# A full-precision decoder layer on one core: the eleventh gate-and-up chunk, and a sixth k-pair of the second down pass, by seven block products

## The chip, the cores and the metric

The kernel runs on one core of a Trainium2 chip. The metric is the device time of one execution in microseconds (us): median, lowest and highest of three runs. TensorE is called PE here, VectorE DVE, ScalarE ACT, GpSimd POOL and SyncE SP, as in the profile.

## The reference, cut to what matters

A sequence of 256 tokens with 2048 channels goes through a SwiGLU network, a token mixer and a second SwiGLU network, each followed by a layer norm. Only the two SwiGLU networks are touched here:

```
def swiglu(x, w_gate, w_up, w_down):
    return (jax.nn.silu(x @ w_gate) * (x @ w_up)) @ w_down

h = layer_norm(DEEPNORM_ALPHA * h + 0.5 * swiglu(h, w_gate, w_up, w_down), g, b)
```

`w_gate` and `w_up` are 2048 by 5632, `w_down` is 5632 by 2048, everything in float32.

## The kernel before, in words

**Products.** Each float32 operand is split into a high part and a rest, and a product of two tiles is three matmuls (high by high, high by rest, rest by high; the function `three`, and the three calls in `up_slab`, L882 to L884), each with 128 rows of tokens and 512 columns of weights. A *slab* is a piece of a weight matrix of two k-tiles (256 rows) by 512 columns, 512 KB. Used plainly it takes 2 k-tiles x 2 token tiles x 3 = 12 matmuls.

**Seven products.** Two slabs with the same rows (gate and up, or two neighbouring column blocks of the down matrix) make, with the two k-tiles and the two token tiles, a 2 by 2 block product. It can be had with seven products instead of eight: 21 matmuls for a pair of slabs where the plain way has 24 (`seven_products`). For that DVE forms three sums of weight tiles (`block_sums`, L2020 to L2025), which ACT and DVE split in high and rest (`t_high_part` L1486, `t_low_part` L2031), and four mixes of token tiles, once for a k-pair (`mixed_of` L1979 to L1985, `mixed_high` L1453, `mixed_low` L2011). The seven results go to eight PSUM banks: `own` holds results by column and token tile, `aux` four partial results, which DVE adds in when the last block is done: `copy_one` and `collect` (L2037 to L2039), `sum_chunk` (L1955, L1957), `product_summed` (L1962) for a chunk, `copy_one_down` and `collect_down` (L2106 to L2114) for a down pass.

**The stages.** Gate and up go over 11 chunks of 512 hidden columns, 16 slabs each. `acc` and `spare`, four banks each, take turns as a chunk's `own`. Chunk 0 is plain, chunks 1 to 9 (`NC_S` = 9) have k-pairs 2, 4 and 6 by seven products (`up_seven`), and chunk 10 is plain (`up_plain`). After a chunk DVE multiplies silu(gate) by up, PE transposes the product (`turn_hidden`, eight small matmuls at L895) and ACT and DVE split it into `g_hi` and `g_lo` (L1432, L1970). The down projection then goes over the 22 k-pairs of the hidden columns in two passes (j = 0 and 1), each for two blocks of 512 output columns, so 44 slabs; `DOWN_ORDER` gives the order of the k-pairs and `DOWN_SEVEN` = 11, 13, 15, 17, 19 those by seven products in both passes. In pass 0 these stand in the last half, slabs 22 to 41; in pass 1 they alternate with plain pairs from slab 8 on. Both networks run the same code (f = 1 and 2).

**What sets the order.** The program of each engine is written out by slab number l. SP loads slab l into one of four landing places as soon as DVE is done with slab l - 4 (L507). ACT copies it to `w_hi` (L1343) when it has landed and PE is done with slab l - 4. DVE forms `w_lo` (L1787), and PE waits for that. All other work of ACT and DVE stands in front of the split of some slab. In down pass 0 DVE has, in front of the split of the slab named:

- slab 3: the product of chunk 10 (`product_plain`, L1949); slab 7: `hidden_low`
- slabs 10, 12, 14, 16: one quarter of the residual. In the first network it is one multiplication (L2142), in the second `prepare_rows` (L1871, L1873), which waits for quarters and for `rows`, the gain and bias of a layer norm, both loaded by POOL
- slabs 11, 13, 15, 17, 19: `mixed_down`, the mix of one of the five k-pairs, behind the `mixed_low` of the one before; slab 21: the last `mixed_low`

POOL loads the residual again once its space, which holds the chunks' partial sums, is free: the upper half when the last seven-product chunk is summed (`refill_late`, L655), the lower half when the last chunk is transposed (L659, L739). In the second network it loads `rows` between the two (L627, L628), at the end of chunk 10.

Of the kernel before, what the change touches and what calls it, by code (L numbers as in the profile page):

```python
# [90 lines left out]
DOWN_SLABS = [[(p, 1 - c if DOWN_ORDER[j][p] in DOWN_SEVEN else c) for p, c in DOWN_SLABS[j]] for j in range(2)]  # L91
UP_BLOCKS = NC_S * len(SEVEN)
ALL_BLOCKS = UP_BLOCKS + 2 * len(DOWN_SEVEN)
# [110 lines left out]
def down_block(f, j, q):  # L204
    return (f - 1) * ALL_BLOCKS + UP_BLOCKS + j * len(DOWN_SEVEN) + q

# [67 lines left out]
def build_decoder_layer(nc, x, positions, ffn1_w_gate, ffn1_w_up, ffn1_w_down, ln1_g, ln1_b, w_in, conv_w, conv_b,  # L274
# [20 lines left out]
    with ctx:  # L295

        land_all = sb("land", [P, 3 + LAND * 2, W])
        t_sums = land_all[:, 0:3, :]
        land = land_all[:, 3:3 + LAND * 2, :].rearrange("p (r k) n -> p r k n", r=LAND)
# [13 lines left out]
        def placed(name, shape, dt, at):  # L313
# [40 lines left out]
        sz = sb("sz", [P, TOK, W])  # L354
        bcT = sb("bcT", [P, 2, SEQ])
# [32 lines left out]
        t_of = {"up": (t_hi, t_lo), "down": (d_t_hi, d_t_lo)}  # L388
# [104 lines left out]
        def _(sp):  # L493
# [28 lines left out]
            def up_rest(f, phase):  # L522
                with sp.Fori(1, NC_S + 1) as i:
                    up_seven(f, phase, i)
                for i in range(NC_S + 1, NC_F):
                    up(f, phase, i)
# [219 lines left out]
        def _(pe):  # L746
# [157 lines left out]
            def seven_products(n, slab_at, l, rows_of, mixed, t_set, own, aux, first, last, turned=None):  # L904
# [7 lines left out]
                def t_block(m):  # L912
                    hi, lo = t_of[t_set]
                    return hi[:, m, :], lo[:, m, :]
# [14 lines left out]
            def up_seven_block(f, i, b, own, aux):  # L929
# [3 lines left out]
                def rows_of(k, t):  # L933
# [3 lines left out]
                               (s_hi[s], s_lo[s]), "up", own, aux, s == 0, s == len(SEVEN) - 1,  # L937
# [17 lines left out]
            def down_seven_block(f, j, l, own, aux):  # L955

                s = DOWN_ORDER[j][DOWN_SLABS[j][l][0]]
                q = DOWN_SEVEN.index(s)

                def rows_of(k, t):  # L960
                    return tuple(m[:, 2 * s + k, t * P:(t + 1) * P] for m in (g_hi, g_lo))

                if j == 0:
                    pe.wait_ge(mix_out, (f - 1) * MIXED + len(SEVEN) + q + 1)
                seven_products(down_block(f, j, q), slab_no(f"down{f}", j, l), l, rows_of, d_s[q], "down",
                               own, aux, q == 0, q == len(DOWN_SEVEN) - 1)

            def down(f):

                for j in range(2):  # L970
                    own, aux = chunk_banks(1 - j), chunk_banks(j)
                    if j == 0:
                        pe.wait_ge(gt_out, 2 * chunk_no(f, NC_F - 1))
                    else:
                        pe.wait_ge(aux_out, shared_down(f, 0) + 1)
                    for l, (p, c) in enumerate(DOWN_SLABS[j]):
# [5 lines left out]
                        if s in DOWN_SEVEN:  # L982
# [19 lines left out]
            def banks_drained(f, i):  # L1002
# [4 lines left out]
                n = shared_no(f, NC_S) + 1 if isinstance(i, int) and i > NC_S else shared_no(f, i)  # L1007
# [25 lines left out]

            def up_plain(f, i):

                for l in range(16):
                    if l == 0:
                        banks_drained(f, i)
                    if l == 4:
                        turn_hidden(f, i - 1, (i - 1) % 2)  # L1040
                    up_slab(f"up{f}", i, l, l % 8, l // 8, chunk_banks(i % 2), l % 8 == 0, l % 8 == 7)
# [16 lines left out]
            def ffn(f, ln, x_no):  # L1058
# [10 lines left out]
                for i in range(NC_S + 1, NC_F):  # L1069
                    up_plain(f, i)  # L1070
# [263 lines left out]
        def _(act):  # L1334
# [134 lines left out]
            def up_plain(f, i):  # L1469
                for l in range(16):  # L1470
                    if i == NC_S + 1 and l == 1:
                        copy_one(f, i - 1, (i - 1) % 2)
                    if i == NC_S + 1 and l == 4:
                        silu_summed(f, i - 1)
                    if l == 6:
                        hidden_high(f, i - 1, (i - 1) % 2)
                    if l == 10:
                        silu_plain(f, i)
                    split(f"up{f}", i, l)

            def t_high_part(n, t_set):
# [4 lines left out]
                act.activation(t_of[t_set][0][:, :, :], t_sums, ACT.Copy).then_inc(t_high, 1)  # L1486
# [6 lines left out]
            def up_seven(f, i, odd):  # L1493

                for l in range(16):
# [10 lines left out]
                    if n is not None and l % 2 == 1:  # L1506
                        t_high_part(n, "up")

            def ffn(f, ln, cols):
# [6 lines left out]
                for i in range(NC_S + 1, NC_F):  # L1516
                    up_plain(f, i)
                down(f)

            def copy_one_down(f, j):  # L1520

                act.wait_ge(t_used, down_block(f, j, len(DOWN_SEVEN) - 1) + 1)
# [4 lines left out]
            def down(f):  # L1527
                for j in range(2):
                    for l, (p, c) in enumerate(DOWN_SLABS[j]):
                        s = DOWN_ORDER[j][p]  # L1530
                        if j == 0 and l == 6:
                            hidden_high(f, NC_F - 1, (NC_F - 1) % 2)
                        if j == 0 and l in (13, 15, 17, 19, 21):
                            mixed_high(f, len(SEVEN) + (l - 13) // 2)
                        if (j, l) == (1, 0):
                            copy_one_down(f, 0)
                        if (j, l) == (1, 30):
                            copy_one_down(f, 1)
                        n = down_block(f, j, DOWN_SEVEN.index(s)) if s in DOWN_SEVEN else None
# [3 lines left out]
                        if n is not None and l % 2 == 1:  # L1543
                            t_high_part(n, "down")
# [236 lines left out]
        def _(dve):  # L1781
# [216 lines left out]
            def mixed_down(f, q):  # L1998

                s = DOWN_SEVEN[q]  # L2000
                if q == 0:
                    dve.wait_ge(gt_out, 2 * chunk_no(f, NC_F - 1))
                    dve.wait_ge(t_rest, (f - 1) * ALL_BLOCKS + UP_BLOCKS)
                at = slice(2 * s, 2 * s + 2)
# [22 lines left out]
            def t_low_part(n, t_set):  # L2027

                hi, lo = t_of[t_set]
                dve.wait_ge(t_high, n + 1)  # L2030
                dve.tensor_tensor(lo[:, :, :], t_sums, hi[:, :, :].bitcast(F32), ALU.subtract).then_inc(t_rest, 1)  # L2031
# [27 lines left out]
            def up_plain(f, i):  # L2059
                for l in range(16):  # L2060
                    if i == NC_S + 1:
                        if l == 1:
                            collect(f, i - 1, (i - 1) % 2)
                        if l == 3:
                            sum_chunk(f, i - 1, (i - 1) % 2)
                        if l == 4:
                            product_summed(f, i - 1)
                    elif l == 2:
                        product_plain(f, i - 1)
                    if l == 7:  # L2070
                        hidden_low(f, i - 1, (i - 1) % 2)
                    split(f"up{f}", i, l)

            def up_seven(f, i, odd):
                for l in range(16):
# [21 lines left out]
                    if l // 2 in SEVEN and l % 2 == 1:  # L2097
                        t_low_part(seven_block(f, i, l // 2), "up")
# [29 lines left out]
            def down(f):  # L2128
                phase = f"down{f}"
                for j in range(2):  # L2130
                    for l, (p, c) in enumerate(DOWN_SLABS[j]):
                        s = DOWN_ORDER[j][p]
                        if j == 0 and l == 3:
                            product_plain(f, NC_F - 1)
                        if j == 0 and l == 7:
                            hidden_low(f, NC_F - 1, (NC_F - 1) % 2)
                        if j == 0 and l in (10, 12, 14, 16):
                            at = (2, 3, 0, 1)[(l - 10) // 2]
# [6 lines left out]
                        if j == 0 and l in (11, 13, 15, 17, 19, 21):  # L2145
# [476 lines left out]
```

## Time and profile before

| | |
|---|---|
| median of 3 runs | 2660.63 us (2659.67 to 2660.86) |
| the profiled execution | 2659.08 us, of which the span is 2657.5 us |
| mean granted TensorE clock | 0.998 |
| PE, DVE, ACT busy | 99%, 75%, 51% of the span |
| gate and up, then down, first network | from the start to about 718 us |
| gate and up, then down, second network | about 1938 us to the end |

PE is busy nearly all the time and the others are not. "Busy" counts a matmul from its issue to its modelled end, 0.39 us, while the next starts after 0.227 us; so a pause of PE of under 0.16 us does not show as idle time, and of a longer one 0.16 us are missing. The median of the runs is 1.55 us above the profiled execution.

### The profile page before, as it was taken

What the parts mean: (1) busy time and instruction counts of PE and PEld (TensorE: products, weight loads), DVE (VectorE), ACT (ScalarE), POOL (GpSimd) and SP (SyncE); (2) the same over time, 40 slices, a digit from 0 to 9 for tenths busy, and PEclk for the clock granted to TensorE, in tenths of its full rate; (3) what the DMA queues carried; (4) which work ended last, traced back from release to release, by engine and by line L of the source; (5) the groups of instructions that cost most, each with busy time, mean ns of one, the idle gap of its engine ahead of it and who ended that gap; (6) DMA issues with size and microseconds to landing.
All of it is one profiled execution on the core that took longest, in us unless ns stands there. A gap on an engine that the chain in (4) does not pass through costs nothing.

```text
span 2657.5 us, 36251 instructions
## 1 busy us (share of the span) xinstructions
PE 2634.0 (99%) x12570; PEld 2187.5 (82%) x12570; DVE 1982.3 (75%) x2254; ACT 1352.8 (51%) x1636; POOL 129.5 (5%) x170
## 2 busy tenths in 40 slices
PE   9999999999999999999999999999999999999997
PEld 7888888888887788888888888888888888888886
DVE  6988987688666665677777765444788989877886
ACT  4555555454444554566555554444365555554553
POOL 1000000000000000211111100000000000000000
PEclk9999999999999999999999999999999999999999
DMA  7666566666655546665555555667666666666664
GB/s 225 202 193 205 190 199 212 212 200 198 204 171 150 152 149 198 206 182 179 178 178 174 181 180 165 191 191 247 202 211 200 191 204 195 200 203 230 212 205 171
DMA packets 286466, 513.95 MB, mean 193 GB/s; under 512 B 19664, under 2 KB 53120, under 8 KB 284320
## 3 DMA queue, kind: packets, MB, share of 16 engines
q1 hardware_dynamic: 279824, 485.03, 58.5%
q0 software_dynamic: 4880, 25.36, 2.6%
q10 hardware_dynamic: 1664, 2.26, 0.2%
q8 instruction: 61, 1.00, 0.1%
q14 instruction: 37, 0.30, 0.0%
HBM read 506.23 MB, written 6.36 MB: 193 GB/s over the span
## 4 chain that ended last, share of the span: by engine, by line
PE 96%; DVE 3%; ACT 1%; issue 0%; DMA 0%; POOLq 0%; ACTq 0%; POOL 0%; SPq 0%; DVEq 0%
PE acc L796 13%; PE acc L798 13%; PE acc L797 13%; PE acc L900 5%; PE acc L901 5%; PE acc L902 5%; PE acc L882 5%; PE acc L884 5%; PE acc L883 5%; PE spare L900 4%; PE spare L902 4%; PE spare L901 4%; PE spare L882 3%; PE spare L884 3%; PE spare L883 3%; PE spare L765 2%
## 5 line engine op out<-in xcount | busy, mean ns | idle before, releaser
L1787 DVE TENSOR_TENSOR w_lo<-land,w_hi 128x1024 fp32r<-128x1024 f32 (+1 forms) x956 | 1152.3, 1222 | 517.7 <-ACT w_hi L1343 509.2
L1343 ACT ACTIVATE w_hi<-land 128x1024 fp32r<-128x1024 f32 (+1 forms) x956 | 967.4, 1026 | 927.9 <-PE acc L798 320.4
L796 PE MATMUL acc<-w_hi,a_hi 128*128 128x512 f32 (+1 forms) x1168 | 443.9, 380 | 1.0 <-DVE w_lo L1787 0.8
L798 PE MATMUL acc<-w_hi,a_lo 128*128 128x512 f32 (+1 forms) x1168 | 428.9, 367 | 0.0
L797 PE MATMUL acc<-w_lo,a_hi 128*128 128x512 f32 (+1 forms) x1168 | 427.5, 366 | 0.0
L796 PEld LDWEIGHTS acc<-w_hi,a_hi 128*128 128x128 f32 x1168 | 220.4, 189 | 44.7 <-issue 10.0
L798 PEld LDWEIGHTS acc<-w_hi,a_lo 128*128 128x128 f32 x1168 | 220.2, 189 | 37.5
L797 PEld LDWEIGHTS acc<-w_lo,a_hi 128*128 128x128 f32 x1168 | 220.7, 189 | 36.5 <-issue 3.6
L882 PE MATMUL acc<-w_hi,a_hi 128*128 128x512 f32 x560 | 220.0, 393 | 0.8 <-DVE w_lo L1787 0.7
L884 PE MATMUL acc<-w_hi,a_lo 128*128 128x512 f32 x560 | 218.2, 390 | 0.0
L883 PE MATMUL acc<-w_lo,a_hi 128*128 128x512 f32 x560 | 217.9, 389 | 0.0
L882 PE MATMUL spare<-w_hi,a_hi 128*128 128x512 f32 x400 | 156.5, 391 | 0.0
L884 PE MATMUL spare<-w_hi,a_lo 128*128 128x512 f32 x400 | 155.7, 389 | 0.0
L883 PE MATMUL spare<-w_lo,a_hi 128*128 128x512 f32 x400 | 155.7, 389 | 0.0
L882 PEld LDWEIGHTS acc<-w_hi,a_hi 128*128 128x128 f32 x560 | 105.1, 188 | 23.4 <-DVE w_lo L1787 1.1
L884 PEld LDWEIGHTS acc<-w_hi,a_lo 128*128 128x128 f32 x560 | 105.1, 188 | 22.2
L883 PEld LDWEIGHTS acc<-w_lo,a_hi 128*128 128x128 f32 x560 | 105.2, 188 | 21.2
L900 PE MATMUL spare<-w_hi,g_hi 128*128 128x512 f32 x292 | 114.0, 390 | 0.6 <-DVE w_lo L1787 0.6
L900 PE MATMUL acc<-w_hi,g_hi 128*128 128x512 f32 x292 | 113.7, 389 | 0.0
L901 PE MATMUL spare<-w_lo,g_hi 128*128 128x512 f32 x292 | 113.6, 389 | 0.0
L902 PE MATMUL spare<-w_hi,g_lo 128*128 128x512 f32 x292 | 113.6, 389 | 0.0
L902 PE MATMUL acc<-w_hi,g_lo 128*128 128x512 f32 x292 | 113.6, 389 | 0.0
(388 smaller groups left out, 4264.7 us busy)
## 6 DMA issues: line engine op xcount, KB each, us to landing
land<-w_in SPq DMA_DIRECT2D x232, 512.0 KB, 3.8
land<-ffn_w_gate SPq DMA_DIRECT2D x176, 512.0 KB, 4.0
land<-ffn_w_up SPq DMA_DIRECT2D x176, 512.0 KB, 4.1
land<-ffn_w_down SPq DMA_DIRECT2D x176, 512.0 KB, 4.5
land<-w_ssd_o SPq DMA_DIRECT2D x64, 512.0 KB, 4.0
land<-w_in SPq DMA_DIRECT2D x132, 128.0 KB, 2.3
land<-w_attn_o SPq DMA_DIRECT2D x32, 512.0 KB, 4.2
land<-w_out SPq DMA_DIRECT2D x32, 512.0 KB, 4.6
```

Of the source, the lines that this page charges most:

```text
L765: return pe.transpose(spare[0:src.shape[-1], bank, at:at + rows], src, ident[0:rows, 0:rows])
L796: pe.matmul(to, rows_hi, hi, start=first, stop=False)
L797: pe.matmul(to, rows_hi, lo, start=False, stop=False)
L798: mm = pe.matmul(to, rows_lo, hi, start=False, stop=last)
L882: pe.matmul(to, rows_hi, hi, start=first and k == 0, stop=False)
L883: pe.matmul(to, rows_hi, lo, start=False, stop=False)
L884: mm = pe.matmul(to, rows_lo, hi, start=False, stop=last and k == 1)
L900: pe.matmul(to, rows[0], block[0], start=first, stop=False)
L901: pe.matmul(to, rows[0], block[1], start=False, stop=False)
L902: return pe.matmul(to, rows[1], block[0], start=False, stop=last)
L1343: act.activation(w_hi[:, l % SPLIT, 0:deep, 0:width], land[:, l % LAND, 0:deep, 0:width], ACT.Copy).then_inc(high, 1)
L1787: dve.tensor_tensor(w_lo[:, l % SPLIT, 0:deep, 0:width], land[:, l % LAND, 0:deep, 0:width], w_hi[:, l % SPLIT, 0:deep, 0:width].bitcast(F ...
```

## The change

Chunk 10 also takes k-pairs 2, 4 and 6 by seven products (`NC_S` = 10), so no plain chunk is left behind the loop. Its partial results are collected, summed and multiplied in down pass 0, in front of the splits of slabs 1, 3 and 4, and PE waits for the collection before slab 0 of the pass, whose banks it fills. The down projection gets a sixth k-pair by seven products, k-pair 10, in pass 1 alone; it takes place 14 in the order, slabs 28 and 29, and its mix is formed in front of slab 5 of pass 1, with the `mixed_low` in front of slab 7. Pass 1's partial results are collected in front of slab 34 instead of 30. In pass 0 the four quarters of the residual move from slabs 10, 12, 14, 16 to 12, 14, 16, 18. The upper half of the residual is loaded again after the sum of chunk 10 and no longer in chunk 10. The split weight sums have one pair of buffers, `t_hi` and `t_lo`, for both stages, outside the shared region; in return `sz` and `bcT` lie on the sums' own space. The six mixes of the down projection lie at 88 to 112 K. Constants and places:

```diff
-NC_S = 9
-DOWN_SEVEN = (11, 13, 15, 17, 19)
-DOWN_ORDER = (tuple(range(22)), (0, 1, 2, 3, 11, 4, 13, 5, 15, 6, 17, 7, 19, 8, 9, 10, 12, 14, 16, 18, 20, 21))
+NC_S = 10
+DOWN_SEVEN = (11, 13, 15, 17, 19, 10)
+DOWN_BLOCKS = (5, 6)
+DOWN_ORDER = (tuple(range(22)), (0, 1, 2, 3, 11, 4, 13, 5, 15, 6, 17, 7, 19, 8, 10, 9, 12, 14, 16, 18, 20, 21))
+DOWN_COLLECT = 34
+MIX_FIRST, MIX_LATE = 11, 5
...
-ALL_BLOCKS = UP_BLOCKS + 2 * len(DOWN_SEVEN)
+ALL_BLOCKS = UP_BLOCKS + sum(DOWN_BLOCKS)
...
+        sz = land_all[:, 0:2, :]
+        bcT = land_all[:, 2, :].rearrange("p (k n) -> p k n", k=2)
...
-        sz = sb("sz", [P, TOK, W])
-        bcT = sb("bcT", [P, 2, SEQ])
...
-        t_hi = placed("t_hi", [P, 3, W], F32R, 36 * K)
-        t_lo = placed("t_lo", [P, 3, W], F32R, 80 * K)
+        t_hi = sb("t_hi", [P, 3, W], F32R)
+        t_lo = sb("t_lo", [P, 3, W], F32R)
...
-               for k, at in enumerate((88, 92, 108, 112, 116))]
-        d_t_hi = placed("d_t_hi", [P, 3, W], F32R, 96 * K)
-        d_t_lo = placed("d_t_lo", [P, 3, W], F32R, 102 * K)
+               for k, at in enumerate((88, 92, 96, 100, 104, 108))]
```

On PE, in `down` and `down_seven_block` (`up_plain` goes):

```diff
                     if j == 0:
                         pe.wait_ge(gt_out, 2 * chunk_no(f, NC_F - 1))
+                        pe.wait_ge(aux_out, shared_no(f, NC_S) + 1)
...
-                if j == 0:
-                    pe.wait_ge(mix_out, (f - 1) * MIXED + len(SEVEN) + q + 1)
+                pe.wait_ge(mix_out, (f - 1) * MIXED + len(SEVEN) + q + 1)
```

On ACT, in `down`:

```diff
-                        if j == 0 and l == 6:
-                            hidden_high(f, NC_F - 1, (NC_F - 1) % 2)
-                        if j == 0 and l in (13, 15, 17, 19, 21):
-                            mixed_high(f, len(SEVEN) + (l - 13) // 2)
+                        if j == 0 and l == 1:
+                            copy_one(f, NC_S, NC_S % 2)
+                        if j == 0 and l == 4:
+                            silu_summed(f, NC_S)
+                        if j == 0 and l == HIDDEN_AT:
+                            hidden_high(f, NC_S, NC_S % 2)
+                        if j == 0 and l in range(MIX_FIRST + 2, MIX_FIRST + 2 * DOWN_BLOCKS[0] + 2, 2):
+                            mixed_high(f, len(SEVEN) + (l - MIX_FIRST - 2) // 2)
+                        if j == 1 and l == MIX_LATE + 2:
+                            mixed_high(f, len(SEVEN) + DOWN_BLOCKS[0])
...
-                        if (j, l) == (1, 30):
+                        if (j, l) == (1, DOWN_COLLECT):
                             copy_one_down(f, 1)
```

On DVE, in `down`:

```diff
+                        if j == 0 and l == 1:
+                            collect(f, NC_S, NC_S % 2)
                         if j == 0 and l == 3:
-                            product_plain(f, NC_F - 1)
-                        if j == 0 and l == 7:
-                            hidden_low(f, NC_F - 1, (NC_F - 1) % 2)
-                        if j == 0 and l in (10, 12, 14, 16):
-                            at = (2, 3, 0, 1)[(l - 10) // 2]
+                            sum_chunk(f, NC_S, NC_S % 2)
+                        if j == 0 and l == 4:
+                            product_summed(f, NC_S)
+                        if j == 0 and l == HIDDEN_AT:
+                            hidden_low(f, NC_S, NC_S % 2)
+                        if j == 0 and l in (12, 14, 16, 18):
+                            at = (2, 3, 0, 1)[(l - 12) // 2]
...
+                        if (j, l) == (1, MIX_LATE):
+                            mixed_down(f, DOWN_BLOCKS[0])
+                        if (j, l) == (1, MIX_LATE + 2):
+                            mixed_low(f, len(SEVEN) + DOWN_BLOCKS[0])
...
-                        if (j, l) == (1, 30):
+                        if (j, l) == (1, DOWN_COLLECT):
                             collect_down(f, 1)
```

## Rows read from the trace of the kernel before

**Rows 1.** The page: busy time of each engine, share of the span, instructions.

```profile
PE 2634.0 (99%) x12570; PEld 2187.5 (82%) x12570; DVE 1982.3 (75%) x2254; ACT 1352.8 (51%) x1636; POOL 129.5 (5%) x170
```

**Rows 2.** Who PE waited for, 2400 us to the end: in total, times, longest (us).

```profile
PE spare L900 <- DVE w_lo L1787: 0.6, 1, 0.6
```

**Rows 3.** Timeline of PE: first matmuls of chunks 8, 10, down pass 0 (f = 1).

```profile
355.05 0.39 PE L882 MATMUL acc<-w_hi,a_hi 128*128 128x512 f32 x1
...
439.83 0.39 PE L882 MATMUL acc<-w_hi,a_hi 128*128 128x512 f32 x1
...
484.27 0.39 PE L900 MATMUL spare<-w_hi,g_hi 128*128 128x512 f32 x1
```

**Rows 4.** Busy time by stretch: us, then PE, PEld, DVE, ACT, POOL, PEclk, DMA share, GB/s.

```profile
2280.00:2320.00 40.00, 40.00 (x182) 33.17 (x181) 35.97 (x35) 21.74 (x22) 0.00 (x0) 1.00 0.64 201
2412.00:2416.00 4.00, 4.00 (x21) 3.32 (x20) 1.97 (x2) 1.06 (x1) 0.00 (x0) 1.00 0.99 412
```

**Rows 5.** Timeline of DVE at the start of chunk 10 (f = 1): start, us.

```profile
436.66 1.22 DVE L2039 TENSOR_TENSOR resid<-acc,resid 128x1024 f32<-128x1024 f32 x1
...
440.07 1.21 DVE L1955 TENSOR_TENSOR resid<-resid,spare 128x1024 f32<-128x1024 f32 x1
441.20 1.21 DVE L1957 TENSOR_TENSOR resid<-resid,spare 128x1024 f32<-128x1024 f32 x1
...
443.59 1.22 DVE L1962 TENSOR_TENSOR resid<-resid 128x1024 f32<-128x1024 f32 x1
```

**Rows 6.** Timeline of DVE in down pass 0 (f = 2), slabs 9 to 18.

```profile
2426.01 1.23 DVE L1787 TENSOR_TENSOR w_lo<-land,w_hi 128x1024 fp32r<-128x1024 f32 x1 [1.49 <-ACT w_hi L1343]
2427.16 1.22 DVE L1871 SCALAR_TENSOR_TENSOR resid<-resid,rows 128x1024 f32<-128x1024 f32 x1
...
2429.67 1.23 DVE L1787 TENSOR_TENSOR w_lo<-land,w_hi 128x1024 fp32r<-128x1024 f32 x1
2430.81 0.68 DVE L1979 TENSOR_TENSOR sz<-g_hi,g_lo 128x512 f32<-128x512 f32 x1
...
2432.53 1.22 DVE L1787 TENSOR_TENSOR w_lo<-land,w_hi 128x1024 fp32r<-128x1024 f32 x1
...
2437.31 0.68 DVE L2011 TENSOR_TENSOR d_lo<-sz,d_hi 128x512 fp32r<-128x512 f32 x1
...
2439.75 1.22 DVE L1787 TENSOR_TENSOR w_lo<-land,w_hi 128x1024 fp32r<-128x1024 f32 x1
...
2454.21 2.35 DVE L1787 TENSOR_TENSOR w_lo<-land,w_hi 128x1024 fp32r<-128x1024 f32 x2
```

**Rows 7.** Timeline of PE (f = 2): start of down pass 0, and around slab 17.

```profile
2407.45 0.39 PE L900 MATMUL spare<-w_hi,g_hi 128*128 128x512 f32 x1
...
2454.53 0.39 PE L902 MATMUL spare<-w_hi,g_lo 128*128 128x512 f32 x1
2455.48 0.50 PE L900 MATMUL spare<-w_hi,g_hi 128*128 128x512 f32 x1 [0.56 <-DVE w_lo L1787]
2455.82 0.40 PE L901 MATMUL spare<-w_lo,g_hi 128*128 128x512 f32 x1
```

**Rows 8.** Timeline at slab 22 (f = 2): DVE's sums and split, PE's first seven-product block.

```profile
2463.97 1.23 DVE L2020 TENSOR_TENSOR land<-land 128x1024 f32<-128x1024 f32 x1 [0.96 <-DMA land<-ffn_w_down]
2466.57 2.35 DVE L1787 TENSOR_TENSOR w_lo<-land,w_hi 128x1024 fp32r<-128x1024 f32 x2
...
2469.21 0.39 PE L900 MATMUL spare<-w_hi,d_hi 128*128 128x512 f32 x1
```

**Rows 9.** DMA issues, 2405 to 2430 us: count, KB each, median us to landing.

```profile
land<-ffn_w_down SPq DMA_DIRECT2D x8, 512.0 KB, 5.9
rows<-ln_g POOLq DMA_DIRECT2D x1, 1024.0 KB, 7.4
rows<-ln_b POOLq DMA_DIRECT2D x1, 1024.0 KB, 10.0
```

**Rows 10.** Timeline of DVE: residual in pass 0 (f = 1); slab 6 of pass 1 (f = 2).

```profile
503.98 0.68 DVE L2142 TENSOR_SCALAR resid<-resid 128x1024 f32<-128x1024 f32 x1
...
2535.16 1.23 DVE L1787 TENSOR_TENSOR w_lo<-land,w_hi 128x1024 fp32r<-128x1024 f32 x1 [1.08 <-ACT w_hi L1343]
```

More of the change, by code:

```diff
@@ L902, in three, with seven_products @@
                 return pe.matmul(to, rows[1], block[0], start=False, stop=last)
-            def seven_products(n, slab_at, l, rows_of, mixed, t_set, own, aux, first, last, turned=None):
+            def seven_products(n, slab_at, l, rows_of, mixed, own, aux, first, last, turned=None):
                 def block(l, k):
@@ L936, in up_seven_block @@
                 seven_products(seven_block(f, i, b), slab_no(f"up{f}", i, 2 * b), 2 * b, rows_of,
-                               (s_hi[s], s_lo[s]), "up", own, aux, s == 0, s == len(SEVEN) - 1,
+                               (s_hi[s], s_lo[s]), own, aux, s == 0, s == len(SEVEN) - 1,
                                chunk_no(f, i) * 2 if s == 0 else None)
@@ L961, in rows_of @@
                     return tuple(m[:, 2 * s + k, t * P:(t + 1) * P] for m in (g_hi, g_lo))
-                if j == 0:
-                    pe.wait_ge(mix_out, (f - 1) * MIXED + len(SEVEN) + q + 1)
-                seven_products(down_block(f, j, q), slab_no(f"down{f}", j, l), l, rows_of, d_s[q], "down",
-                               own, aux, q == 0, q == len(DOWN_SEVEN) - 1)
+                pe.wait_ge(mix_out, (f - 1) * MIXED + len(SEVEN) + q + 1)
+                seven_products(down_block(f, j, q), slab_no(f"down{f}", j, l), l, rows_of, d_s[q],
+                               own, aux, q == 0, q == DOWN_BLOCKS[j] - 1)
             def down(f):
@@ L1006, in banks_drained @@
                     pe.wait_ge(gt_out, n)
-                n = shared_no(f, NC_S) + 1 if isinstance(i, int) and i > NC_S else shared_no(f, i)
+                n = shared_no(f, i)
                 if not is_zero(n):
@@ L1467, in up_first, with t_high_part @@
                     split(phase, 0, l)
[L1469 to L1481, printed above, removed]
+            def t_high_part(n):
                 act.wait_ge(sums, n * 3 + 3)
@@ L1485, in t_high_part @@
                     act.wait_ge(t_used, n)
-                act.activation(t_of[t_set][0][:, :, :], t_sums, ACT.Copy).then_inc(t_high, 1)
+                act.activation(t_hi[:, :, :], t_sums, ACT.Copy).then_inc(t_high, 1)
             def copy_one(f, i, odd):
@@ L1515, in ffn @@
                         up_seven(f, m * 2 + (ALONE - 1 + k), (ALONE + 1 + k) % 2)
[L1516 to L1517 removed]
                 down(f)
             def copy_one_down(f, j):
[L1522 removed]
+                act.wait_ge(t_used, down_block(f, j, DOWN_BLOCKS[j] - 1) + 1)
                 if j == 1:
@@ L1543, in down @@
                         if n is not None and l % 2 == 1:
-                            t_high_part(n, "down")
+                            t_high_part(n)
             ffn(1, "xT", None)
@@ L2057, in up_first @@
                 mixed_low(f, len(SEVEN) - 1)
[L2059 to L2072, printed above, removed]
             def up_seven(f, i, odd):
@@ L2164, in down @@
                         if n is not None and l % 2 == 1:
-                            t_low_part(n, "down")
+                            t_low_part(n)
                 evacuate_down(f, 1, 0)
```

49 lines of the change are left out of this document (19 added, 30 removed).

## The prediction, made before the changed kernel ran

> **What bounds the kernel now.** I read the page first: PE is busy 99% of the span, DVE 75%, ACT 51% [rows 1]. Then the list of waits. In the second network's last chunk and both its down passes PE waited once, 0.6 us, for DVE's `w_lo` [rows 2]. Then the timeline of PE. Chunks 8 and 9, seven-product chunks, take 439.83 - 355.05 = 84.78 us, 42.39 each; plain chunk 10 takes 484.27 - 439.83 = 44.44 [rows 3]. A plain chunk has 16 x 12 = 192 large matmuls, a seven-product one 5 x 24 + 3 x 21 = 183, and both have eight transposes. So nine matmuls make 2.05 us, 0.228 each, and PE sets the time. DVE is close behind: in a stretch of seven-product chunks it is busy 35.97 of 40 us and PE all 40 [rows 4]. So the questions are how many matmuls go, and whether DVE stays ahead where work is put on it.
>
> **How far DVE is ahead.** DVE can be no more than four slabs ahead, since `w_hi` of slab l waits for PE to be done with slab l - 4. In down pass 0 of the second network it waits for ACT, and ACT for PE, up to slab 9 (split at 2426.01, 1.49 us idle before it), and is free at 2427.16 [rows 6]. PE starts slab 0 at 2407.45 and slab 17 would have started at 2454.53 + 0.23 = 2454.76 [rows 7], so it reaches slab 9 eight slabs of 2.72 us earlier, at 2433.0. DVE's lead is thus 5.8 us when full. From there it falls.
>
> **Removed.** Per network: three blocks in chunk 10 and one in pass 1, each three matmuls. That is 2 x (3 + 1) x 3 = 24 matmuls. Six blocks in chunk 10 are 2 x 2.05 = 4.10 us; six matmuls in pass 1 at 0.228 are 1.36. Sum 5.46 us. Bounds: 24 matmuls at 0.226 to 0.230 give 5.4 to 5.5.
>
> The rule that speaks against this size is in the Trainium skill, TensorE: Matmul & The Clock Gate, section Back-to-back issue gap. It gives 131 ns for a sustained matmul of 512 columns, about 216 ns for an isolated one; by these the 24 would be worth, as an estimate, 3.1 or 5.2 us. The trace disagrees with both.
>
> **Added in chunk 10 and at the head of pass 0.** DVE gets the block sums of chunk 10 (three times the pattern of rows 8: 2.60 us of sums and a split of the sums), then the collection, two sums and the product. All this is what it does in chunks 1 to 9, where PE loses nothing [rows 4]: the first sum starts 0.24 us after PE enters the next stage (440.07 against 439.83) and the product ends at 444.8 [rows 3, 5]. PE wants the product for the transposes in front of slab 3, 3 x 2.72 = 8.2 us after its entry, so 3.2 us are left. The new wait of PE in front of slab 0 is for the collection, whose last instruction ends at 437.88, 2.0 us before PE would stop [rows 3, 5]. Behind that wait stands all of PE's work, so late here is late one for one; but the last plain pair of chunk 10 (5.4 us) covers it as it covers chunks 1 to 9. Cost 0, bounds 0 and 0.3. By slab 9 the lead is full again, since plain slabs leave DVE 1.5 us each [rows 6].
>
> **The middle of pass 0, second network.** This is the term that costs. Steps, from rows 6: a split takes DVE 1.14 us (2429.67 to 2430.81). A quarter of the residual with its split takes 2429.67 - 2427.16 + 1.14 = 3.65. The first mix with its split takes 2432.53 - 2430.81 + 1.14 = 2.86. A later one, with the `mixed_low` before it, takes 2439.75 - 2437.31 + 1.14 = 3.58. PE takes 2.72 for each.
> Before, DVE has quarters at 10, 12, 14, 16 and mixes at 11, 13, 15, 17: 28.3 us from 2427.16, so the split of slab 17 ends at about 2455.43 where PE wanted it at 2454.76. PE starts at 2455.48 and its next matmul follows after 0.34 instead of 0.23 us [rows 7], 0.85 us lost. From 18 on there is no quarter and DVE recovers.
> After, the quarters are at 12, 14, 16, 18 and the mixes stay. Slab 10 is split on the beat and leaves DVE free at 2426.01 + 2.72 + 1.14 = 2429.87. To the end of slab 18 it has 2.86 + 4 x 3.65 + 3 x 3.58 = 28.2 us, hence 2458.1, and 0.1 for the split's own end; PE wants slab 18 at 2457.48 and loses 0.85. Then slab 19 has another mix: 3.58 against 2.72, 0.86 lost again. Sum 1.7, against 0.85 before: **0.87 us more.** In both networks the number of such instructions is the same; what is new is that the last mix follows the last quarter directly.
> At slab 22 the block sums wait for a landing [rows 8]. Slab 23 can be asked for only when slab 19 is split, so with DVE at its latest this chain moves too: split 22 ended at about 2467.8 for a PE start at 2469.21, 1.4 us to spare; sums move by 1.5 us, PE by 0.87, which leaves 0.8. Cost 0, bounds 0 and 0.8, if the landing takes as much longer as it did under load.
> Bounds of this whole term: 0 and 1.7. In the first network a quarter is one instruction of 0.68 us [rows 10], so a quarter and a mix take 0.72 + 1.14 + 3.58 = 5.44 us for two slabs, which is PE's time: 0.
>
> **Pass 1.** The mix of k-pair 10 adds 1.72 us in front of slab 5 and its `mixed_low` 0.7 in front of slab 7. At slab 6 DVE waits for ACT, that is for PE, 1.08 us, and at slab 7 again [rows 10]; the lead of some 5 us covers both. Cost 0, without that cover up to 2.4 a network. The collection at 34 stands four slabs behind its last block, as at 30 before. 0.
>
> **POOL's transfers.** The upper half of the residual (1 MB) is now asked for about 2 us into pass 0, in front of `rows` (2 MB); all wait for SP's stream too. In the second network they share 412 GB/s [rows 4], of which the slabs, 0.524 MB each 2.72 us, need 193. `rows` landed 7.4 and 10.0 us after their issue [rows 9]. One more MB at some 210 GB/s is 5 us: the last row would land at about 2426, before DVE wants it at slab 12, at 2432.7. Cost 0. SP's slabs took a median of 5.9 us to land there [rows 9] and made nobody wait. SP's and ACT's other steps only change place.
>
> **Sum.** -5.46 + 0.87 = -4.6 us. Profiled execution 2659.08 to about 2654.5 (span 2652.9); median of the runs 2660.63, 1.55 above it, to **2656.0**. That is 0.17% faster, inside the 0.2% (5.3 us) that a measurement of this kernel can tell from no change.
>
> **Rivals.**
> *The full saving.* DVE makes up the second late mix, or the landing of the quarters lets it start sooner. For it: only 0.87 us are at stake. Against it: the steps of rows 6 are the same every time. Time 2655.2, a bare 0.2% faster. Chance 0.14.
> *Pauses in the first blocks too.* The landing for slab 23 comes late, and DVE, busy at 90%, gains only some tenths of a microsecond a block, so that two or three pauses follow. Price 1 to 3 us over the forecast: 2657 to 2659. For it: 0.96 us idle for a landing already [rows 8]. Chance 0.14.
> *Slower.* The late quarters or `rows` aren't there at slab 12. From there DVE has no slack, so each us is lost by PE. To be slower by 5.3 us, `rows` must land at about 2432.7 + 9.9 = 2442.6, that is POOL's 3.1 MB must move at under 100 GB/s from 2411. At 90 GB/s they land at 2446: -5.46 + 0.87 + 13.8 = +9.2, 2669.8. Against it: 412 - 193 = 219 GB/s went to POOL's transfers [rows 4]. Chance 0.02. The Trainium skill, DMA: Bandwidth & Descriptors, section Queues, rings and completion order, says that an engine takes its queues in turn, a packet from each; by that POOL's queue can't be starved.
> *It doesn't do what it says.* Then no block is gained and the time stays; the diff leaves no room for it. Chance 0.01.
>
> **How the numbers follow.** Forecast 0.69. Range 2654.7 to 2658.3: below, the full saving and the runs' own spread of 0.6; above, 1.7 us for the middle of pass 0 and a pause at slab 22. Faster by over 0.2% needs 2655.3: most of the full saving and a little of the forecast's edge, 0.16. Slower 0.03. Same 0.81.
>
> **What would show it.** PE with 24 large matmuls fewer; chunk 10 at 42.4 us in both networks; pass 0 of the first network unchanged; in the second network two waits for `w_lo` of about 0.6 us each, at slabs 18 and 19; none at slab 0 of the passes, and none in pass 1. The forecast is wrong if PE waits at the head of pass 0 or at slab 22, or if DVE waits for a DMA at slab 12.

## The result, and the profile after

The changed kernel is slower: 2666.26 us median (2664.71 to 2668.9, 13 runs) against 2660.86 (2659.43 to 2661.8, 13 runs) for the kernel before on the same chip, ratio 1.0021, 95% interval 1.0013 to 1.003. Its profiled execution has a span of 2664.0 us, 6.5 more than before. The page's busy line, as in [rows 1]:

```profile
PE 2637.0 (99%) x12546; PEld 2183.1 (82%) x12546; DVE 2027.2 (76%) x2306; ACT 1365.7 (51%) x1648; POOL 130.1 (5%) x170
```

The 24 matmuls are gone (12570 to 12546), and PE is nevertheless busy 3.0 us longer. The timeline of PE at the first matmuls of chunks 8 and 10 and of down pass 0, first network, as in [rows 3] (here and below, `...` stands for rows left out):

```profile
356.83 0.39 PE L885 MATMUL acc<-w_hi,a_hi 128*128 128x512 f32 x1
...
442.13 0.39 PE L885 MATMUL acc<-w_hi,a_hi 128*128 128x512 f32 x1
...
484.80 0.39 PE L903 MATMUL spare<-w_hi,g_hi 128*128 128x512 f32 x1
```

Chunk 10 did fall, from 44.44 to 42.67 us. But chunks 8 and 9 rose, from 42.39 each to 42.65, though the diff touches none of their work. The same view inside chunk 9, from the first matmul that reads the weight sums to one 19 matmuls later, first the kernel before, then the changed one:

```profile
411.95 0.39 PE L900 MATMUL acc<-t_hi,s_hi 128*128 128x512 f32 x1
...
416.25 0.39 PE L883 MATMUL spare<-w_lo,a_hi 128*128 128x512 f32 x1
```

```profile
413.76 0.39 PE L905 MATMUL spare<-w_hi,a_lo 128*128 128x512 f32 x1
413.99 0.40 PE L903 MATMUL acc<-t_hi,s_hi 128*128 128x512 f32 x1
414.23 0.40 PE L904 MATMUL acc<-t_lo,s_hi 128*128 128x512 f32 x1
...
418.38 0.39 PE L886 MATMUL spare<-w_lo,a_hi 128*128 128x512 f32 x1
```

4.30 us have become 4.39. No idle time stands in these rows; the starts are just a little further apart, 0.24 us at the first read of `t_hi` where 0.227 is usual. Averaged over the chunks it is 0.087 us a block. There are 30 + 5 + 6 blocks per network, 82 in all: 7.1 us.

The list of waits of PE from 2400 us to the end, as in [rows 2], and the pauses themselves in PE's timeline, as in [rows 7]:

```profile
PE spare L903 <- DVE w_lo L1770: 3.1, 6, 0.6
```

```profile
2409.74 0.39 PE L903 MATMUL spare<-w_hi,g_hi 128*128 128x512 f32 x1
...
2432.85 0.50 PE L903 MATMUL spare<-w_hi,g_hi 128*128 128x512 f32 x1 [0.30 <-DVE w_lo L1770]
...
2452.68 0.50 PE L903 MATMUL spare<-w_hi,g_hi 128*128 128x512 f32 x1 [0.45 <-DVE w_lo L1770]
...
2467.14 0.50 PE L903 MATMUL spare<-w_hi,g_hi 128*128 128x512 f32 x1 [0.53 <-DVE w_lo L1770]
```

One pause at slab 8 of the pass, and five at slabs 15 to 19 (three of them between the last two rows shown), where I forecast two, at slabs 18 and 19. The timeline of ACT and of DVE shows what was late before the first of them:

```profile
2426.53 1.06 ACT L1334 ACTIVATE w_hi<-land 128x1024 fp32r<-128x1024 f32 x1 [5.97 <-DMA land<-ffn_w_down]
2430.48 1.06 ACT L1334 ACTIVATE w_hi<-land 128x1024 fp32r<-128x1024 f32 x1 [2.89 <-DMA land<-ffn_w_down]
```

```profile
2427.62 1.23 DVE L1770 TENSOR_TENSOR w_lo<-land,w_hi 128x1024 fp32r<-128x1024 f32 x1 [5.80 <-ACT w_hi L1334]
2431.57 3.75 DVE L1770 TENSOR_TENSOR w_lo<-land,w_hi 128x1024 fp32r<-128x1024 f32 x3 [2.72 <-ACT w_hi L1334]
2435.24 0.68 DVE L1962 TENSOR_TENSOR land<-g_hi,g_lo 128x512 f32<-128x512 f32 x1
```

ACT and DVE stood idle for landings of weights. Before, ACT waited between 2405 and 2435 us for PE and for no landing, and DVE for ACT or PE. The DMA issues of 2405 to 2430 us, as in [rows 9], and the window in which the queues are full, as in [rows 4]:

```profile
land<-ffn_w_down SPq DMA_DIRECT2D x7, 512.0 KB, 11.1
resid<-kept POOLq DMA_DIRECT2D x2, 1024.0 KB, 9.9
rows<-ln_g POOLq DMA_DIRECT2D x1, 1024.0 KB, 10.9
rows<-ln_b POOLq DMA_DIRECT2D x1, 1024.0 KB, 13.7
```

```profile
2421.00:2425.00 4.00, 4.00 (x19) 3.30 (x19) 0.82 (x1) 0.00 (x0) 0.00 (x0) 1.00 1.03 419
```

POOL asks for 4 MB between 2411.75 and 2419.23 us, within the first slabs of the pass. A slab of weights, landed after 5.9 us before, took 11.1. The queues of the same 25 us, with packets, MB and share, first of the kernel before, then of the changed one (q1 carries SP's weights, q0 POOL's transfers):

```profile
q1 hardware_dynamic: 2408, 4.66, 53.8%
q0 software_dynamic: 560, 3.15, 33.7%
```

```profile
q0 software_dynamic: 832, 4.19, 44.6%
q1 hardware_dynamic: 1826, 3.52, 39.8%
```

POOL moved 1.04 MB more and SP 1.14 MB less, 141 GB/s where the slabs need 193. SP asks for a slab only when DVE is done with the one four before, and four slabs are 10.9 us of PE's time, so with landings of 11 us and more there is nothing left for ACT and DVE, and DVE's lead shrinks. PE still found 4.00 us of work in that window, so the list of PE's waits names no DMA: the price is paid later, when DVE, without its lead, reaches the slabs with extra work.

**The account by stages.** From the same matmul to the same matmul, after less before: start -0.03, gate and up 0.55, pass 0 0.43, pass 1 -0.16, the mixer between the networks 0.94, gate and up 0.55, pass 0 4.38, pass 1 with the end -0.16; together 6.5. By causes: matmuls -5.46, the blocks' 0.087 us times 82 = 7.1, the second late mix 0.87, the late landings 3.1 (the rest of pass 0), the mixer 0.9. The mixer's 0.9 I take for no effect of the change: in the experiments below whose tiles don't slow the mixer (all but 6, 10 and 11), the same stage came out -0.1 to 1.1 us longer than in that one profile of before, with the old code too (0.7 in run 4).

### The profile page after: what moved, and what is told of

Read it like the earlier page. It is cut to its first block, busy times and chain, and to the rows that moved or that the text cites. A ratio compares the mean times of both kernels' runs of the same rounds, so it can differ in the third digit from the quotient of the medians.

```text
span 2664.0 us, 36358 instructions
## 1 busy us (share of the span) xinstructions
PE 2637.0 (99%) x12546; PEld 2183.1 (82%) x12546; DVE 2027.2 (76%) x2306; ACT 1365.7 (51%) x1648; POOL 130.1 (5%) x170
## 4 chain that ended last, share of the span: by engine, by line
PE 95%; DVE 3%; ACT 1%; DMA 1%; issue 0%; ACTq 0%; POOLq 0%; POOL 0%; SPq 0%; DVEq 0%
PE acc L799 13%; PE acc L801 13%; PE acc L800 13%; PE acc L903 5%; PE acc L905 5%; PE acc L904 5%; PE spare L903 4%; PE spare L905 4%; PE spare L904 4%; PE acc L885 4%; PE acc L887 4%; PE acc L886 4%; PE spare L885 3%; PE spare L887 3%; PE spare L886 3%; PE spare L768 2%
## 5 line engine op out<-in xcount | busy, mean ns | idle before, releaser
L799 PEld LDWEIGHTS acc<-w_hi,a_hi 128*128 128x128 f32 x1168 | 220.4, 189 | 45.8 <-issue 11.0
L801 PEld LDWEIGHTS acc<-w_hi,a_lo 128*128 128x128 f32 x1168 | 220.2, 189 | 37.5
L800 PEld LDWEIGHTS acc<-w_lo,a_hi 128*128 128x128 f32 x1168 | 220.7, 189 | 36.6 <-issue 3.6
L885 PE MATMUL acc<-w_hi,a_hi 128*128 128x512 f32 x512 | 202.2, 395 | 0.6 <-DVE w_lo L1770 0.6
L887 PE MATMUL acc<-w_hi,a_lo 128*128 128x512 f32 x512 | 200.2, 391 | 0.0
L886 PE MATMUL acc<-w_lo,a_hi 128*128 128x512 f32 x512 | 199.3, 389 | 0.0
L2015 DVE TENSOR_TENSOR t_lo<-land,t_hi 128x1536 fp32r<-128x1536 f32 x82 | 143.5, 1750 | 0.2 <-ACT t_hi L1465 0.2
L1465 ACT ACTIVATE t_hi<-land 128x1536 fp32r<-128x1536 f32 x82 | 121.0, 1476 | 0.0
L885 PEld LDWEIGHTS acc<-w_hi,a_hi 128*128 128x128 f32 x512 | 96.1, 188 | 21.3 <-DVE w_lo L1770 0.9
L887 PEld LDWEIGHTS acc<-w_hi,a_lo 128*128 128x128 f32 x512 | 96.1, 188 | 21.3
L886 PEld LDWEIGHTS acc<-w_lo,a_hi 128*128 128x128 f32 x512 | 96.2, 188 | 20.0
```

Of the source, the lines that this page charges most:

```text
L799: pe.matmul(to, rows_hi, hi, start=first, stop=False)
L800: pe.matmul(to, rows_hi, lo, start=False, stop=False)
L801: mm = pe.matmul(to, rows_lo, hi, start=False, stop=last)
L885: pe.matmul(to, rows_hi, hi, start=first and k == 0, stop=False)
L886: pe.matmul(to, rows_hi, lo, start=False, stop=False)
L887: mm = pe.matmul(to, rows_lo, hi, start=False, stop=last and k == 1)
```

## The experiments

Times below are each kernel's median beside that of the kernel before, measured together with it. That was 2660.39 us for runs 1 to 4 and 2660.52 for runs 5 to 8.

**1. The new places alone.** The kernel before, with `sz` and `bcT` on the sums' space, by the lines of the change, and the sums of gate and up at the end:

```diff
-        t_hi = placed("t_hi", [P, 3, W], F32R, 36 * K)
-        t_lo = placed("t_lo", [P, 3, W], F32R, 80 * K)
+        t_hi = sb("t_hi", [P, 3, W], F32R)
+        t_lo = sb("t_lo", [P, 3, W], F32R)
```

> The kernel before with the buffers of the changed kernel and nothing else: t_hi and t_lo of the gate-and-up stage at the end of the memory, sz and bcT on the space of the sums; the down stage keeps its own pair in the shared region. Theory (the new place of t_hi and t_lo slows PE by 0.087 us in each seven-product block that reads them): 54 blocks x 0.087 = 4.7 us slower than before, chunks of 42.65 instead of 42.39 us, the ten down blocks of each network as fast as before. Rival (the slower chunks come from the changed order of the work, not from the place): no change, chunks of 42.39 us. If the pause of 1.2 us before the first matmuls of the mixer comes from sz on the sums, it is here too and makes it 5.9.

2665.13 us (2664.17 to 2666.01), ratio 1.0017 (1.0008 to 1.0027). The timeline of PE, first matmuls of chunks 8 and 10:

```profile
357.59 0.39 PE L882 MATMUL acc<-w_hi,a_hi 128*128 128x512 f32 x1
...
442.89 0.39 PE L882 MATMUL acc<-w_hi,a_hi 128*128 128x512 f32 x1
```

(442.89 - 357.59) / 2 = 42.65. No instruction was added or removed; 54 blocks at 0.087 are 4.7 us, measured 4.7. The new places alone cost this, without the new order of the work; which of the moved tiles it is, run 5 tells.

**2. Another 64 bytes.** The changed kernel with `sb("pad", [P, 16])` in front of `t_hi`, so that both tiles start at a multiple of 128 bytes:

> The changed kernel with 64 bytes put in front of t_hi, so that t_hi and t_lo start at a multiple of 128 bytes (as they did before, and as w_hi and w_lo do) but stay at the end of the memory. Theory of alignment: all seven-product blocks lose their 0.087 us, 82 x 0.087 = 7.1 us faster than the changed kernel, about 2 us faster than before. Rival (it is the distance or the high address): no change against the changed kernel, 5.4 us slower than before.

2665.24 us (2664.13 to 2666.6), ratio 1.0018 (1.0008 to 1.0027); chunks 42.63. Alignment to 128 bytes doesn't mend it.

**3. POOL's transfers one by one.** The changed kernel, second network. It asks for three transfers within 1.3 us and for the fourth 6.2 us later; here three of the four wait for slabs 2, 4 and 6 of the pass:

```diff
-            pool.wait_ge(used, slab_no("up2", NC_F - 1, 15) + 1)
-            load_rows(rows, ln2_g, ln2_b, rows_in)
+            pool.wait_ge(used, slab_no("down2", 0, 2) + 1)
+            pool.dma_start(rows[:, 0, :], ln2_g[0, :].partition_broadcast(P)).then_inc(rows_in, 16)
+            pool.wait_ge(used, slab_no("down2", 0, 4) + 1)
+            pool.dma_start(rows[:, 1, :], ln2_b[0, :].partition_broadcast(P)).then_inc(rows_in, 16)
             hidden_complete(2)
+            pool.wait_ge(used, slab_no("down2", 0, 6) + 1)
```

> The changed kernel with POOL's four loads of the second network's down pass 0 spaced out, so that about one is under way at a time (the two rows and the lower half of the residual wait for PE to be done with slabs 2, 4 and 6). Theory (the burst of 4 MB kept the weight slabs back by up to 14 us and took DVE's lead before the quarters began): slabs land in under 9 us, no pause at slab 8, two pauses instead of five at slabs 15 to 19, 3 us faster than the changed kernel (about 2.4 us slower than before). Rival (DVE is simply too busy there whatever lands): no gain.

2662.84 us (2661.6 to 2663.46), ratio 1.0008 (0.9998 to 1.0017). PE's timeline has exactly two pauses in the pass. Behind them, the DMA issues of 2405 to 2430 us with the landings, and DVE's first mix:

```profile
2461.13 0.50 PE L906 MATMUL spare<-w_hi,g_hi 128*128 128x512 f32 x1 [0.65 <-DVE w_lo L1773]
...
2464.70 0.50 PE L906 MATMUL spare<-w_hi,g_hi 128*128 128x512 f32 x1 [0.56 <-DVE w_lo L1773]
```

```profile
land<-ffn_w_down SPq DMA_DIRECT2D x8, 512.0 KB, 6.6
```

```profile
2432.80 0.68 DVE L1965 TENSOR_TENSOR land<-g_hi,g_lo 128x512 f32<-128x512 f32 x1
```

From its first matmul to that of pass 1, pass 0 fell from 122.58 to 119.50 us, by 3.1. DVE began its first mix 2432.80 - 2410.37 = 22.4 us after PE's first matmul of the pass, as the prediction had it (2429.87 - 2407.45 = 22.4), and in the changed kernel 2435.24 - 2409.74 = 25.5. The landings took 3.1 us of its lead, and PE lost as much.

**4. The burst alone.** The kernel before, with the wait for the last slab of chunk 10 put in front of the upper half of the residual instead of behind it, so that all is asked for together:

```diff
-            refill_late(2, kept_view)
             pool.wait_ge(used, slab_no("up2", NC_F - 1, 15) + 1)
+            refill_late(2, kept_view)
```

> The kernel before with one change: in the second network the upper half of the residual is loaded again only after the last slab of chunk 10, so that all 4 MB of POOL's loads fall in the first slabs of down pass 0, as in the changed kernel. Theory (the burst costs by itself): slabs land 12 us or more after their issue, and pass 0 takes 1.5 to 4 us longer than before. Rival (the fourth MB costs nothing, as the prediction had it): within 0.3 us of before.

2665.43 us (2663.55 to 2666.63), ratio 1.0017 (1.0007 to 1.0027): 5.0 us, more than I expected. Pass 0 took 4.88 more. The waits of PE from 2400 us on:

```profile
PE spare L900 <- DVE w_lo L1787: 3.8, 7, 0.6
```

Seven pauses, at slabs 8 and 12 to 17. In the kernel before the quarters begin at slab 10, two slabs earlier than in the changed one, so that DVE has less time to recover from late landings; that this makes the difference between 4.9 and 3.1 us is argued and not shown.

**5. The sums low.** The changed kernel with `t_hi` and `t_lo` where `resid` was (59520 and 65664 bytes into each partition, that is from 58 KiB on; what I expected of run 12 says 54) and `resid` at the end:

> The changed kernel with t_hi and t_lo next to w_lo at the low end of the memory and resid, which PE reads only for transposes, at the end in their place. Theory (PE loses 0.087 us in each block whose weight sums it reads from the end of the memory): chunks of 42.39 us again, 82 x 0.087 = 7.1 us faster than the changed kernel, about 1.7 us faster than before. Rival (it comes from t_hi and t_lo being a pair shared by both stages, or from sz on the sums' space): chunks stay at 42.65 us, no gain.

2659.65 us (2657.48 to 2664.99), ratio 0.9998 (0.9989 to 1.0008). Chunks are back at 42.39, pass 1 is 0.67 us shorter than before, in both networks; only pass 0 of the second still pauses, five times. So the tiles' place, and not their sharing or the blocks' number, made the 7 us. (The median moved by a little less, from 5.4 us above the kernel before to 0.9 below it.) `resid`, which PE reads only in the small transposes, lies at the end without harm.

**6. `w_lo` last.** The kernel before, with `w_lo`, which a third of all large matmuls read, allocated behind all other tiles:

> The kernel before with w_lo, which every third large matmul reads, at the end of the memory (from about 206 KB on) and all else 16 KB lower. If any tile at the end of the memory costs PE some 5 ns for each matmul that reads it and for those that follow, some 3500 matmuls give 18 us or more slower than before, in plain chunks too. If only the tiles of the sums are touched by it, within 1 us of before.

2702.86 us (2701.99 to 2703.43, 4 runs), ratio 1.0159 (1.0143 to 1.0174). Here the matmuls on `w_hi`, whose own place is low, are slower too: on plain slabs of pass 0, first network, their mean steps are 0.231 to 0.233 us, like those on `w_lo`.

**7. Both cures,** edits 3 and 5 together:

> The changed kernel with both: t_hi and t_lo at the low end, and POOL's loads in the second network spaced out. Theory: -5.46 us of matmuls and +0.87 of the two pauses are left, as the prediction had them: 4.6 us faster than before. Rival (the two costs overlap, so that taking both away gives less than the sum): 1 to 3 us faster than before.

2655.49 us (2654.8 to 2656.48), ratio 0.998 (0.9971 to 0.9989). Pass 0 has the two pauses of the prediction:

```profile
2454.39 0.51 PE L906 MATMUL spare<-w_hi,g_hi 128*128 128x512 f32 x1 [0.64 <-DVE w_lo L1773]
...
2457.97 0.50 PE L906 MATMUL spare<-w_hi,g_hi 128*128 128x512 f32 x1 [0.52 <-DVE w_lo L1773]
```

The same profile has one pause that nobody forecast, in pass 1 right behind the new block, at slab 30, where ACT had waited 5.88 us for a landing:

```profile
2601.11 0.50 PE L906 MATMUL acc<-w_hi,g_hi 128*128 128x512 f32 x1 [0.71 <-DVE w_lo L1773]
```

It cost 1.0 us, and this execution was the slowest of the eleven. No other profile with the new order has it, and its cause is open.

**8. The mixes four slabs earlier,** on top of 7: `MIX_FIRST = 7`, so that the last mix no longer follows the last quarter:

> As the kernel before it, with the five mixes of down pass 0 from slab 7 on instead of 11, so that the last three no longer stand between the last quarters of the residual. DVE's deficit from slab 11 to 18 is then 3 x 0.86 + 4 x 0.93 - 0.86 = 5.4 us against a lead of 5.8: no pause in pass 0 of either network, not even the one of the kernel before. 5.46 + 0.85 = 6.3 us faster than before. Rival (the lead isn't full at slab 11, since the weight slabs land late beside POOL's loads): one or two pauses stay, 4.6 to 5.5 us faster.

2653.77 us (2652.77 to 2656.05), ratio 0.9974 (0.9965 to 0.9984). PE waits for nobody in the stretch of [rows 2]; ACT's longest waits there are for PE again, as the list of its waits from 2405 to 2435 us shows:

```profile
ACT w_hi L1337 <- PE spare L908: 9.4, 7, 1.9
ACT w_hi L1337 <- DMA land<-ffn_w_down: 2.4, 2, 1.2
```

This version beats both kernels: 6.75 us under the one before and, by the two differences to it, 12.2 under the changed one.

**9. Where it begins.** The kernel before with `w_lo` moved right behind the region, to bytes 190592 to 206976 (one run, as in 10 and 11):

> The kernel before with w_lo moved from the front of the memory to 190.6 to 207.0 KB of each partition, right behind the shared region (which moves down by 16 KB); in the run with w_lo behind all other tiles it lay at about 206 to 222 KB and the kernel took 42 us longer. Theory one, only the very last part of the memory is slow to read: seven-product chunks stay at 42.39 us, plain ones at 44.44, total 2660 within 2. Rival, the slowness grows with the address or with the distance of w_lo from w_hi: chunks of 42.6 or more and a total of 2668 or more. In the kernel before, the rests of the activations (a_lo) lie in this same stretch and cost nothing, which speaks for theory one.

2659.96 us, before 2660.97. At this place nothing is lost. I took it for a border above 207 KB.

**10 and 11. The border.** The same with a pad in front of `w_lo`, to 196608 to 212992, and, with `sz` and `bcT` ahead of it as well, to 200704 to 217088:

> The kernel before with w_lo at 196608 to 212992 bytes of each partition, so that it ends at 208 KiB. Measured so far: 190592 to 206976 costs nothing, 206272 to 222656 costs 42 us and lengthens every matmul of plain slabs from 0.2267 to 0.2320 us. Theory one: the slow part begins at 208 KiB (212992) or above. Then total 2660 within 2, pass 0 of the first network 109.0. Rival: it begins below 208 KiB, between 206976 and 212992. Then chunks over 42.5 and a total of 2665 to 2703.

> The kernel before with w_lo at 200704 to 217088 bytes, so that its fourth slot alone (slabs 3, 7, 11, ...) lies above 208 KiB. Theory one, each read above the border costs, and its effect lasts some matmuls longer: one slab in four slow in whole or in most, total 2660 plus 10 to 25. Rival, one tile above the border slows all matmuls of the kernel alike: 2700 or more, every slab 2.784 instead of 2.72 us. Third, the border lies above 217088: 2660 within 2; the sums' tiles at 216512 to 228800 don't contradict that.

2692.17 and 2693.19 us, before 2661.18: 31 and 32 us. The timeline of PE over 120 matmuls on plain slabs of pass 0, first network, in run 9, then in run 10:

```profile
500.08 0.39 PE L900 MATMUL spare<-w_hi,g_hi 128*128 128x512 f32 x1
...
527.27 0.39 PE L900 MATMUL spare<-w_hi,g_hi 128*128 128x512 f32 x1
```

```profile
500.42 0.39 PE L901 MATMUL spare<-w_hi,g_hi 128*128 128x512 f32 x1
...
528.15 0.39 PE L901 MATMUL spare<-w_hi,g_hi 128*128 128x512 f32 x1
```

27.19 / 120 = 0.2266 us against 27.73 / 120 = 0.2311; run 11 has the same 0.2311, and in both runs it is the same in all four slots of `w_lo`. Run 10's time by itself is what its rival, a border below 208 KiB, had forecast, but no border above which reads are slow fits all three runs. Run 9's upper half and run 10's lower half are mostly the same bytes (198784 to 204800 in both), once at full speed and once not, and run 11's tax is hardly larger than run 10's. Of the three outcomes I had written down for run 11 none came. What the place of run 9 has in common with the activations is that it starts 128 bytes past a multiple of 2048; runs 10 and 11 start on such a multiple.

**12. The sums right behind the region.** The changed kernel, a single step of order in the allocation:

```diff
         sb("region", [P, 32 * 1024])
+        t_hi = sb("t_hi", [P, 3, W], F32R)
+        t_lo = sb("t_lo", [P, 3, W], F32R)
```

(and not behind the small tiles). They start at 206976 and 213120, both 128 past a multiple of 2048, and still lie above the `w_lo` of run 9.

> The changed kernel with t_hi and t_lo right behind the shared region (206976 and 213120 bytes of each partition) in front of the small tiles, instead of at the very end (216512 and 222656). So far w_lo at 190592 to 206976 costs nothing, at 196608 to 212992 it costs 31 us and at 206272 to 222656 42 us, in all its four slots alike. Theory one, what counts in the upper part is how a tile's start stands to the others: 190592 was 128 bytes past a multiple of 2048, as the activations are, 196608 and 200704 were multiples of 2048. 206976 and 213120 are 128 past one too, so the tax is gone: seven-product chunks at 42.39, total about 2659.6, as with the sums at 54 KiB. Rival, a border: what starts above 190592 and below 196608 or higher is slow wherever it stands. Chunks at 42.65, total about 2666.

2659.41 us (2658.07 to 2660.89), before 2660.36, ratio 0.9997 (0.9987 to 1.0006). The timeline of PE, first matmuls of chunks 8 and 10:

```profile
355.14 0.39 PE L885 MATMUL acc<-w_hi,a_hi 128*128 128x512 f32 x1
...
439.92 0.39 PE L885 MATMUL acc<-w_hi,a_hi 128*128 128x512 f32 x1
```

(439.92 - 355.14) / 2 = 42.39. Gate and up is 2.04 us shorter than before, pass 1 0.67, as in run 5: the tax is gone, at addresses in the middle of those that paid it. The six pauses of pass 0 are still there. So a high place alone doesn't bring the tax. A border that slows all matmuls as soon as one tile lies above it is out too: `t_lo` lies here above the whole of run 10's `w_lo`.

What the tax goes with is seen when the low places are worked out as well. The shared region ends at byte 206976 and is 131072 long, and in front of it stand `resid`, `w_lo` and `w_hi` with 16384 each; so in the kernel before they start at 75904, 59520, 43136 and 26752. All of these are 128 past a multiple of 2048, and so are the activations, the mixes and the old places of the sums inside the region. Every moving or stationary tile of the large matmuls that cost nothing thus had this one offset, low and high (run 5's too), and every tile that brought the tax had another one: 1472 in the changed kernel and in runs 1, 3 and 6, 1536 in run 2, 0 in runs 10 and 11.

## Why the prediction was wrong

**The places of the buffers: not priced at all.** The prediction tells the saving, the work of DVE and the transfers; the part of the diff that moves `t_hi`, `t_lo`, `sz` and `bcT` has no term and no bound. It was worth 7.1 us, more than the whole saving (runs 1, 5 and 12). What the diff changed there is the offset of the split sums' start, from 128 to 1472 bytes past a multiple of 2048. The trace of before held nothing that would have given its size, since all its operands of large matmuls have the one offset. But the sum bounds its other terms, and this one, 738 reads of the sums (82 x 9), got neither a term nor a bound.

**"POOL's transfers ... Cost 0": wrong by 3.1 us.** I asked whether the late rows reach DVE in time, which they did: DVE waited for no row. I did not ask what POOL's 4 MB do to the weights beside them, beyond the remark that their 5.9 us "made nobody wait". 412 GB/s less 193 for the slabs presumes that the slabs keep their 193; they got 141 (3.52 MB in 25 us; with the transfers one by one in run 3 it was 4.38 MB), and their landing went from 5.9 to 11.1 us. I also counted 3.1 MB, and left out the lower half of the residual behind them. The pause it causes is the rival "Pauses in the first blocks too" in kind (a landing is late) but not in place: it was the landings of slabs 7 and 8, not of slab 23. The Trainium skill, DMA: Bandwidth & Descriptors, section Queues, rings and completion order, by which I argued that POOL's queue can't be starved, says just as much that SP's queue gets no precedence. The trace agrees with both: POOL's queue moved 4.19 MB and SP's 3.52 in the same 25 us.

**"The middle of pass 0": right.** 0.87 us more, two pauses (1.30 us in run 3, of which the tax of five blocks is 0.43; 0.90 in run 7). Shown by runs 3 and 7, with 0.65 and 0.56, and 0.64 and 0.52 us idle where 0.6 each was forecast; run 8, which takes the second mix away from the last quarter, takes them all away.

**"Removed": right.** In runs 5, 7, 8 and 12 chunk 10 gains 2.05 a network (42.39 against 44.45) and pass 1 gains 0.68, but for the stray pause of run 7; 5.46 in sum. In runs 5 and 8 the first network's chunk 0 took 0.3 us longer, which hides part of it. **The new wait at the head of pass 0, chunk 10's collection and pass 1: right at 0.** The first network of runs 5 and 7 has pass 0 at +0.01 us in both. Only run 7's one pause in pass 1 speaks against "none in pass 1".

With the two missing terms the sum is -5.46 + 0.87 + 7.1 + 3.1 = +5.6; the medians of the comparison differ by 5.4. Run 7, which has neither, came to 5.03 us under the kernel before where the sum said 4.6. So the forecast failed by two terms set at nothing, and what it did price came out as priced.

## What to carry to other kernels

A buffer that moves is a change of its own: when the time between two matmuls moves by a few nanoseconds with no idle time beside it, compare a stretch that the diff doesn't touch, and try the same kernel with the places alone, keeping in one trial the offset that the other operands' starts have. Here a single reordering of the allocation (run 12) gave back 7 us by the stages, and 6.4 by the medians. And where transfers are bunched, ask not only when they land, but what the stream that was already running then takes to land, and how many microseconds of lead the engine behind it has left when its extra work begins; the wait list will name that engine, not the DMA.

## What the runs showed of the hardware

- PE's steady step for a 128x512 matmul on plain slabs was 0.2267 us. With only `w_lo` moved it was 0.2266 (start at 190592), 0.2311 (196608 or 200704) or 0.2320 (206272). The slow ones were about equally slow for all four slots of `w_lo`, and matmuls that read `w_hi` were slowed as well (in run 10, mean steps of 0.2275 to 0.2342 in all twelve positions of a slab).
- The starts that cost time were 0, 1472 and 1536 bytes past a multiple of 2048 and lay at byte 196608 or above. Those that cost nothing were 128 past one, from 26752 up to 213120, like the starts of all other tiles that the large matmuls read. Three things stay open. The modulus need not be 2048: modulo 256 the costly starts are 0 and 192, the free ones 128. It is not shown whether the offset itself counts or its difference to that of the operand beside it, which was 128 in every run. And no tile with another offset was tried low in the memory.
- The Trainium skill, SBUF — State Buffer, section SBUF size: 192, 224, or 256?, gives some 208 KiB as usable under a scratch area for descriptors. That border is not the cause here: in run 10 `w_lo` ends exactly there and costs 31 us, in run 12 `t_lo` lies above it and costs nothing.
- The same page's section Who interferes with whom says that PE never waits for anyone at its memory ports. No run here shows whom it waits for, but its step does depend on where its operands lie.
- Single executions part at the three small loads (`head_r`) that ACT issues at the mixer's start, the same in every kernel: issuing them took ACT 0.39, 0.47 and 0.53 us in the profile of before, and 0.40, 0.79 and 1.31 us in that of the changed kernel, where PE then stood idle for 1.23 us. In run 4, with the old code, they took 0.39, 0.73 and 1.07, and PE stood idle for 0.92.
